# Stepped weight tiles in the up and gate products, and permuted moving columns in the second block

## The chip, the cores and the metric

The kernel is one program on one core of a Trainium2 chip. The metric is the device time of that program in microseconds; the kernel before was run twice. TensorE (PE) multiplies: a weight load (PEld in the profile) brings 128 columns of a stationary operand into the array, and a matmul streams the moving operand past them into a PSUM bank. ACT (ScalarE) and DVE (VectorE) prepare operands and empty banks, SP issues the DMAs.

## The reference, cut to what matters

Two networks follow one another on 256 tokens of width 2048, in float32: first two layers with mixers, an FFN with a convolution and an embedding gate, then two layers with three kinds of attention. The change touches these products:

```python
# first block, in each of two layers
h = causal_dwconv(x @ w_up, conv_w, conv_b)          # up0, up1: 2048 x 11264
gate, up = jnp.split(h, 2, axis=-1)
y = (jax.nn.gelu(gate) * up) @ w_down                # down0, down1: untouched
x = x + jax.nn.sigmoid(x @ ple_w_gate[layer]) * (p[layer] @ ple_w_proj[layer])   # pg0, pg1: 2048 x 2048
# second block, in each of two layers
proj = jnp.einsum('bsd,de->bse', h, w_in[l])         # in20 then ib0, in21 then ib1
```

## The kernel before, in words

**Layout.** Activations lie with features on the partitions: a matrix of 2048 features is 16 tiles of 128 partitions x 256 tokens. A weight matrix is cut into pieces of 256 output columns; a piece in DRAM is 128 partitions x 4096 words, which are 16 tiles (one per 128 input features) of 256 columns. A piece arrives in one of three slots of `ring` by a DMA of SP. It has two halves of 128 output columns; each half becomes one output tile.

**Precision.** Each f32 operand is split into a high part, rounded to fp32r, and a low part, the remainder. ACT writes the high part of a half (line 1771), DVE the low part (line 2506, a helper that `split` on line 2564 calls). Both read the half's 128 columns out of the 256 of each tile and write them without gaps, so that `WHI[half]` and `WLO[half]` are 16 tiles of 128 x 128 words, one after the other. The input has a high and a low part likewise, `rhi` and `rlo`, which lie apart in SBUF.

**The matmuls.** `wide_half` (from line 821) makes one half. It waits for a free bank and for the half's high part (`w_hi`), then runs 16 matmuls on line 863: the high weights against the high and the low input together, 512 moving columns, which `pair` describes as two runs of 256. The bank's 512 columns take the two sums. It waits for the low part (`w_lo`) and runs 16 matmuls on line 849 (`from_low_weights`): the low weights against the high input, 256 columns, added to the main half of the bank. ACT and DVE then add the two halves of the bank up. In front of each matmul stands the load of its weights; the program writes the two as one `mm`.

**Which halves.** `up0` and `up1` have 44 pieces each, `pg0` and `pg1` 8, `ib0` and `ib1` 17. The first piece of `up` and `pg` goes through `both_halves` instead, because its input arrives in quarters: 96 matmuls of 256 columns on lines 885, 891 and 897. All others of these names go through `wide_half`. For `up` the pieces run in a hardware loop of three (`rounds`). In the second block, small jobs (logits, transposes, attention values) stand between the halves of `ib0` and `ib1`.

**Order.** SP loads a piece as soon as the slot's last reader has signalled (`piece_done`). ACT splits a half as soon as the piece is there and PE has finished the earlier half in that place (`g_done`), DVE follows ACT, PE follows both.

**Other places that the text speaks of.** Line 2811 is a DVE copy of 32 words per partition, each the last of 64 (`XT[..., C - 1]`), so 64 words apart. Line 1555 has attention logits and line 1679 transposes, with 128 moving columns and plain f32 operands; line 1181 has weights of 32 columns.

Of the kernel before, what the change touches and what calls it, by code (L numbers as in the profile page):

```python
# [15 lines left out]
P = 128  # L16
D = 2048
DT = D // P
# [75 lines left out]

EV_TILES = [24, 25, 26] + list(range(8, 16)) + list(range(0, 8)) + list(range(16, 24))
EV_HALVES = 16 + len(EV_TILES)


def place(p):
# [125 lines left out]
def build(nc, dram, out):  # L225
# [38 lines left out]
    with ctx:  # L264
# [280 lines left out]
        def parts_of(name):  # L545

            return (2, 3, 0, 1) if name == "ev_out" else (0, 1, 2, 3)

        def halves_of(name):

            return (DHI, DLO, FC) if name[:4] == "down" else (WHI, WLO, DT)
# [27 lines left out]
        def pair(name, kk):  # L579

            if name[:4] == "down":
                a, b = kk, FT + high_slot(kk)
                return scrv[:, a:b + 1:b - a, :]
            a, b = sorted(at_ // T + kk for at_ in HI_LO[name])
            if name not in SOURCE:
                a, b = a - 2 * X // T, b - 2 * X // T
                return scrv[:, a:b + 1:b - a, :]
            return allv[:, a:b + 1:b - a, :]
# [171 lines left out]
        def _(pe):  # L760
            mm = nc.tensor.matmul
# [59 lines left out]
            def wide_half(name, k, half, i, first=False, count=1):  # L821

                _, rhi, rlo = RHS[name]
                u = wide_unit(name, k, half)
                b = unit_bank(u)
                main, low = sums(b, name)

                pe.wait_ge(bank_free[u % R3], i * 4 + (2 * (u // R3) + 2))
                pe.wait_ge(S["w_hi"], at(HALF0[name] + half + 1, k, i, 2))
                early = 12  # L830

                def from_high(first_, last):
                    for kk in range(first_, last):
                        if kk % 4 == 0:
                            pe.wait_ge(S["r_hi"], 4 * R_SPLIT.index(name) + kk // 4 + 1)
                        mm(main, WHI[half][:, kk, :], rhi[:, kk, :], start=kk == 0, stop=False,
                           skip_group_check=True)

                def from_low(first_, last):
                    for kk in range(first_, last):  # L840
                        if kk % 4 == 0:
                            pe.wait_ge(S["r_lo"], 4 * R_SPLIT.index(name) + kk // 4 + 1)
                        last_ = mm(low, WHI[half][:, kk, :], rlo[:, kk, :], start=False, stop=False,
                                   skip_group_check=True)
                    return last_

                def from_low_weights(first_, last):
                    for kk in range(first_, last):
                        last_ = mm(main, WLO[half][:, kk, :], rhi[:, kk, :], start=False, stop=kk == DT - 1,  # L849
                                   skip_group_check=True)  # L850
                    return last_

                if first:
                    from_high(0, early)
                    from_low(0, early)
                    pe.wait_ge(S["w_lo"], at(HALF0[name] + half + 1, k, i, 2))
                    from_low_weights(0, early)
                    from_high(early, DT)
                    from_low_weights(early, DT)
                    one = from_low(early, DT)  # L860
                else:
                    for kk in range(DT):
                        mm(b[:, :], WHI[half][:, kk, :], pair(name, kk), start=kk == 0, stop=False,  # L863
                           skip_group_check=True)
                    pe.wait_ge(S["w_lo"], at(HALF0[name] + half + 1, k, i, 2))
                    one = from_low_weights(0, DT)
                one.then_inc(S["g_done"], count)

            def both_halves(name, high, low, units):

                n, first = R_SPLIT.index(name), HALF0[name]
                _, rhi, rlo = RHS[name]
                whi, wlo = zip(*(first_weights(name, half) for half in range(2)))
                for u in units:
                    pe.wait_ge(bank_free[u % R3], 2 * (u // R3) + 2)
                pe.wait_ge(S["w_hi"], first + 2)
                pe.wait_ge(S["w_lo"], first + (2 if name in FIRST_SECOND_HALF else 1))

                def tiles_of(part):
                    return range(4 * part, 4 * part + 4)  # L880

                def high_high(half, part):
                    pe.wait_ge(S["r_hi"], 4 * n + part + 1)
                    for kk in tiles_of(part):
                        mm(high[half], whi[half][:, kk, :], rhi[:, kk, :], start=kk == 0, stop=False, skip_group_check=True)

                def low_high(half, part):
                    if half and not part:
                        pe.wait_ge(S["w_lo"], first + 2)
                    for kk in tiles_of(part):  # L890
                        mm(high[half], wlo[half][:, kk, :], rhi[:, kk, :], start=False, stop=kk == DT - 1,
                           skip_group_check=True)

                def high_low(half, part):
                    pe.wait_ge(S["r_lo"], 4 * n + part + 1)
                    for kk in tiles_of(part):
                        one = mm(low[half], whi[half][:, kk, :], rlo[:, kk, :], start=False, stop=kk == DT - 1,
                                 skip_group_check=True)
                    return one

                def from_high(part):
                    for half in range(2):
                        high_high(half, part)
                    for half in range(2):
                        low_high(half, part)

                from_high(0)
                for half in range(2):
                    high_low(half, 0)
                from_high(1)  # L910
                for half in range(2):
                    high_low(half, 1)
                from_high(2)
                high_high(0, 3)
                low_high(0, 3)
                high_low(0, 2)
                high_low(0, 3).then_inc(S["g_done"], 1)
                high_high(1, 3)
                low_high(1, 3)
                high_low(1, 2)  # L920
                high_low(1, 3).then_inc(S["g_done"], 1)
# [2631 lines left out]
    return np.ascontiguousarray(w.transpose(3, 0, 2, 1, 4).reshape(-1, P, kt * cols))  # L3553


def _half_tiled(w):

    w = _tiled(w, 4, 512)
    return np.ascontiguousarray(w.reshape(-1, 2, P, 2048).transpose(0, 2, 1, 3).reshape(-1, P, 4096))
# [11 lines left out]
def _matrices():  # L3571
    f = np.float32
    out = np.zeros((P, NMAT), f)
    i = np.arange(P)

    def put(name, a):
        out[:a.shape[0], MCOL[name]:MCOL[name] + a.shape[1]] = a

    put("ident", np.eye(P, dtype=f))
    put("ones", np.ones((P, P), f))  # L3580
    put("bones", (i[:, None] // 64 == i[None, :] // 64).astype(f))
    put("rswap", (i[:, None] == (i[None, :] ^ 32)).astype(f))
    j = np.arange(C)
    r = i % C
    sel = np.zeros((P, 32), f)
    sel[i, i // 64] = 1
    put("sel", sel)
    put("selt", ((i[:, None] % 32 < 2) & (i[:, None] % 32 == i[None, :] // 64)).astype(f))
    put("mask", np.concatenate([r[:, None] < j[None, :], r[:, None] <= j[None, :]], 1).astype(f))
    put("twice", (r[:, None] == j[None, :]).astype(f))  # L3590
    levels = []
    for lv in range(6):
        s = 1 << lv

        levels.append(((r[:, None] // (2 * s) == j[None, :] // (2 * s)) & (j[None, :] // s % 2 == 1)
                       & (r[:, None] // s % 2 == 0)).astype(f))
    put("lmask", np.concatenate(levels, 1))

    rel = np.arange(384) - 255
    n = np.abs(rel)  # L3600
    large = 8 + sum((n * n >= 64 * (1 << k)).astype(int) for k in range(1, 8))
    bucket = np.where(rel > 0, 16, 0) + np.where(n < 8, n, np.minimum(large, 15))
    put("onehot", (np.arange(32)[:, None] == bucket[None, :]).astype(f))
    return out


def _layout(a):

    ev, od = a["ev_w_in"][0], a["od_w_in"][0]
    d = {}  # L3610
# [70 lines left out]
    }  # L3681
    d["vec"] = np.ascontiguousarray(np.concatenate([part[name] for name, _ in VECS], 1))
    d["mat"] = _matrices()
    d["relb"] = np.ascontiguousarray(a["rel_bias"])
    pos = np.asarray(a["positions_2"]).astype(np.int32)
    d["posi"] = np.ascontiguousarray(np.concatenate([np.repeat(pos[None], P, 0), pos.reshape(2, P).T], 1))
# [19 lines left out]
```

## Time and profile before

| | us |
|---|---|
| the two runs | 3287.78, 3289.35 |
| median | 3288.57 |
| span of the profiled execution, first to last instruction | 3284.6 |
| PE busy in that span | 3232.2 |
| weight loads busy | 2855.1 |
| DVE busy | 2195.8 |
| ACT busy | 1667.5 |

The profile has no other time for the profiled execution than its span; the runs are 3.2 and 4.8 us longer. Busy time is the union of the records of an engine. Matmuls and weight loads are pipelined: a record of some 390 ns is the latency of one matmul, while the next one starts earlier. How fast they follow one another is read from the chain (so many in so many us), not from the mean of one.

### The profile page before, as it was taken

What the parts mean: (1) busy time and instruction counts of PE and PEld (TensorE: products, weight loads), DVE (VectorE), ACT (ScalarE), POOL (GpSimd) and SP (SyncE); (2) the same over time, 40 slices, a digit from 0 to 9 for tenths busy, and PEclk for the clock granted to TensorE, in tenths of its full rate; (3) what the DMA queues carried; (4) which work ended last, traced back from release to release, by engine and by line L of the source; (5) the groups of instructions that cost most, each with busy time, mean ns of one, the idle gap of its engine ahead of it and who ended that gap; (6) DMA issues with size and microseconds to landing.
All of it is one profiled execution on the core that took longest, in us unless ns stands there. A gap on an engine that the chain in (4) does not pass through costs nothing.

```text
span 3284.6 us, 53186 instructions
## 1 busy us (share of the span) xinstructions
PE 3232.2 (98%) x21672; PEld 2855.1 (87%) x21672; DVE 2195.8 (67%) x2836; ACT 1667.5 (51%) x2138; POOL 24.5 (1%) x38
## 2 busy tenths in 40 slices
PE   9999999999999999999999999999999999999998
PEld 8888898888888888888888888888888888888887
DVE  6577767666676456676766666745675767647676
ACT  5574346555554335554555555533564456444563
POOL 0000000000000000011000000000000000000000
PEclk9999999999999999999999999999999999999999
DMA  7352145455444554534445445455544434444342
GB/s 279 143 210 67 57 167 200 181 188 196 179 185 175 184 190 183 190 119 180 164 181 199 182 186 198 159 186 192 188 168 185 171 129 167 186 175 167 129 171 112
DMA packets 47254, 563.64 MB, mean 172 GB/s; under 512 B 5072, under 2 KB 7264, under 8 KB 10720
## 3 DMA queue, kind: packets, MB, share of 16 engines
q1 hardware_dynamic: 47072, 561.06, 45.4%
q8 instruction: 133, 2.18, 0.3%
q14 instruction: 49, 0.40, 0.0%
HBM read 558.92 MB, written 2.12 MB: 171 GB/s over the span
## 4 chain that ended last, share of the span: by engine, by line
PE 90%; DVE 5%; ACT 3%; issue 2%; DMA 0%; SPq 0%; DVEq 0%; ACTq 0%
PE bank L863 40%; PE bank L849 21%; PE bank L968 10%; PE bank L973 5%; PE bank L1002 3%; ACT spl_r L1771 1%; PE bank L1468 1%; DVE ring L2506 1%; PE bank L784 1%; PE bank L788 1%; PE bank L782 1%; DVE spl_r L2506 1%; DVE xb L2506 1%; DVE xa L2506 0%; DVE scr L2506 0%
## 5 line engine op out<-in xcount | busy, mean ns | idle before, releaser
L2506 DVE TENSOR_TENSOR spl_r<-ring,spl_r 128x2048 fp32r<-128x2048 f32 (+2 forms) x429 | 961.3, 2242 | 485.8 <-ACT spl_r L1771 480.8
L863 PE MATMUL bank<-all_r,spl_r 128*128 128x512 f32 x4960 | 1196.6, 393 | 3.2 <-ACT spl_r L1771 3.2
L1771 ACT ACTIVATE spl_r<-ring 128x2048 fp32r<-128x2048 f32 x407 | 779.2, 1915 | 591.0 <-PE bank L849 484.1
L863 PEld LDWEIGHTS bank<-all_r,spl_r 128*128 128x128 f32 x4960 | 914.5, 188 | 189.5 <-issue 8.0
L849 PEld LDWEIGHTS bank<-all_r,spl_r 128*128 128x128 f32 x5008 | 642.1, 191 | 24.2
L849 PE MATMUL bank<-all_r,spl_r 128*128 128x256 f32 x5008 | 650.0, 283 | 0.0
L2506 DVE TENSOR_TENSOR dsp_r<-ring,dsp_r 128x1408 fp32r<-128x1408 f32 x126 | 204.8, 1625 | 206.4 <-ACT dsp_r L1771 206.2
L968 PE MATMUL bank<-scr_r,dsp_r 128*128 128x512 f32 x1386 | 338.8, 392 | 0.0
L1771 ACT ACTIVATE dsp_r<-ring 128x1408 fp32r<-128x1408 f32 x126 | 174.4, 1384 | 283.3 <-PE bank L973 283.1
L968 PEld LDWEIGHTS bank<-scr_r,dsp_r 128*128 128x128 f32 x1386 | 252.5, 189 | 47.4
L863 PE MATMUL bank<-scr_r,spl_r 128*128 128x512 f32 x1152 | 275.8, 391 | 2.9 <-ACT spl_r L1771 2.9
L863 PEld LDWEIGHTS bank<-scr_r,spl_r 128*128 128x128 f32 x1152 | 211.7, 188 | 45.0 <-issue 3.8
L2512 DVE SCALAR_TENSOR_TENSOR xtra<-sumbuf,vec,xtra 128x255 f32<-128x255 f32 (+1 forms) x352 | 170.2, 484 | 102.0 <-ACT xtra L1929 66.7
L973 PEld LDWEIGHTS bank<-scr_r,dsp_r 128*128 128x128 f32 x1386 | 182.9, 191 | 9.8
L1929 ACT ACTIVATE xtra<-sumbuf,vec 128x256 f32<-128x256 f32 x176 | 105.0, 598 | 168.1 <-DVE sumbuf L2506 168.1
L973 PE MATMUL bank<-scr_r,dsp_r 128*128 128x256 f32 x1386 | 185.9, 282 | 0.0
L849 PEld LDWEIGHTS bank<-scr_r,spl_r 128*128 128x128 f32 x1184 | 151.8, 191 | 5.6
L849 PE MATMUL bank<-scr_r,spl_r 128*128 128x256 f32 x1184 | 153.9, 283 | 0.0
L1935 ACT ACTIVATE xtra<-xtra 128x256 f32<-128x256 f32 x88 | 36.9, 419 | 160.5 <-DVE xtra L2512 160.5
L2506 DVE TENSOR_TENSOR sumbuf<-bank,sumbuf 128x256 f32<-128x256 f32 x275 | 114.7, 418 | 3.9 <-ACT sumbuf L1813 3.7
L1813 ACT ACTIVATE sumbuf<-bank 128x256 f32<-128x256 f32 x275 | 100.2, 365 | 15.6 <-PE bank L849 15.6
L2506 DVE TENSOR_TENSOR scr<-xtra 128x256 f32 (+1 forms) x88 | 37.5, 426 | 18.7 <-DVE xtra L2512 18.4
(437 smaller groups left out, 2673.9 us busy)
## 6 DMA issues: line engine op xcount, KB each, us to landing
ring<-in_up SPq DMA_DIRECT2D x88, 2048.0 KB, 7.8
ring<-in_down SPq DMA_DIRECT2D x64, 1408.0 KB, 6.0
ring<-in_ib SPq DMA_DIRECT2D x34, 2048.0 KB, 7.8
ring<-in_pg SPq DMA_DIRECT2D x16, 2048.0 KB, 7.8
ring<-in_out SPq DMA_DIRECT2D x16, 2048.0 KB, 7.9
ring<-in_in SPq DMA_DIRECT2D x12, 2048.0 KB, 7.7
ring<-in_ec SPq DMA_DIRECT2D x11, 2048.0 KB, 8.4
ring<-in_ea SPq DMA_DIRECT2D x8, 2048.0 KB, 10.5
```

The costliest lines, as they stand in the source:

```text
L782: mm(out_, WHI[half][:, kk, :], rhi[:, kk, :], start=kk == tile_order[0], stop=False)
L849: last_ = mm(main, WLO[half][:, kk, :], rhi[:, kk, :], start=False, stop=kk == DT - 1, skip_group_check=True)
L863: mm(b[:, :], WHI[half][:, kk, :], pair(name, kk), start=kk == 0, stop=False, skip_group_check=True)
L968: mm(b[:, :], high[:, kk, :], pair(name, piece * FC + kk), start=piece + kk == 0, stop=False, skip_group_check=True)
L973: one = mm(main, low[:, kk, :], HHI[:, high_slot(piece * FC + kk), :], start=False, stop=piece == 3 and kk == FC - 1, skip_group_check=True)
L1002: one = mm(out, lhsT, rhs, start=n == 0, stop=n == len(terms) - 1)
L1771: A(high[half], w[:, :, half * P:(half + 1) * P], ACT.Copy).then_inc(S["w_hi"], count)
L1813: A(dst, shape(sums(b, name)[1]), ACT.Copy).then_inc(S["low_act"], count)
L1929: one = A(GU[:, k % R3, half, :], SU[:, k % R3, half, :], ACT.Identity, bias=pick(v("cb", col, FT), index(k, i)), scale=pick(v("cw2", col, ...
L1935: A(GU[:, k % R3, 0, :], GU[:, k % R3, 0, :], ACT.Gelu_apprx_tanh).then_inc(S["up_gelu"], 1)
L2506: return V.tensor_tensor(out, a, b, op)
L2512: return V.scalar_tensor_tensor(out=out, in0=a, scalar=s, in1=b, op0=op0, op1=op1)
```

## The change

Weight tiles of four products are stored interleaved. With a step of n, the tiles of a half lie in groups of n, and the columns of one tile are n words apart: word c * n + j of a group is column c of its tile j. `_stepped` lays the weights out so on the host, and `stationary` reads a tile with that step: 2 words in `up0`, 16 in `up1`, 4 in `pg0`, 8 in `pg1`. All other products keep a step of 1. In `ib0` the moving columns and the bank's columns are both taken from last to first, within each run of 256, in all matmuls. In `ib1` the matmuls of 256 columns (the low weights) take columns in fours, first the fours of even number, then those of odd number, in the input and in the bank alike; its matmuls of 512 columns stay.

```diff
+STEPS = {"up0": 2, "up1": 16, "pg0": 4, "pg1": 8}
...
+        def stationary(name, part, kk):
+
+            step = STEPS.get(name, 1)
+            group = part[:, kk - kk % step:kk - kk % step + step, :].rearrange("p x n -> p (x n)")
+            return group[:, kk % step::step]
+
+        def lines(name, ap):
+
+            if name == "ib1":
+                return ap.rearrange("p (m x c) -> p x m c", x=2, c=4)
+            return ap[:, ::-1] if name == "ib0" else ap
+
+        def both_sides(name, b, kk):
+
+            if name != "ib0":
+                return b[:, :], pair(name, kk)
+            return b[:, :].rearrange("p (x t) -> p x t", x=2)[:, :, ::-1], pair(name, kk)[:, :, ::-1]
...
                 def from_low_weights(first_, last):
                     for kk in range(first_, last):
-                        last_ = mm(main, WLO[half][:, kk, :], rhi[:, kk, :], start=False, stop=kk == DT - 1,
-                                   skip_group_check=True)
+                        last_ = mm(lines(name, main), stationary(name, WLO[half], kk), lines(name, rhi[:, kk, :]), start=False,
+                                   stop=kk == DT - 1, skip_group_check=True)
                     return last_
...
                     for kk in range(DT):
-                        mm(b[:, :], WHI[half][:, kk, :], pair(name, kk), start=kk == 0, stop=False,
+                        both, x = both_sides(name, b, kk)
+                        mm(both, stationary(name, WHI[half], kk), x, start=kk == 0, stop=False,
                            skip_group_check=True)
...
                     for kk in tiles_of(part):
-                        mm(high[half], wlo[half][:, kk, :], rhi[:, kk, :], start=False, stop=kk == DT - 1,
+                        mm(high[half], stationary(name, wlo[half], kk), rhi[:, kk, :], start=False, stop=kk == DT - 1,
                            skip_group_check=True)
...
+def _stepped(d):
+
+    for name, step in STEPS.items():
+        n = step
+        w = d[name].reshape(-1, P, 16 // n, n, 2, P)
+        w = w.transpose(0, 1, 2, 4, 5, 3).reshape(-1, P, 16 // n, 2, n, P).transpose(0, 1, 2, 4, 3, 5)
+        d[name] = np.ascontiguousarray(w).reshape(d[name].shape)
```

The other matmuls of `wide_half` and `both_halves` that take weights take them through `stationary` in the same way.

## Rows read from the trace of the kernel before

**Rows 1.** The page: engines, granted clock by slice, chain that ended last
```profile
PE 3232.2 (98%) x21672; PEld 2855.1 (87%) x21672; DVE 2195.8 (67%) x2836; ACT 1667.5 (51%) x2138; POOL 24.5 (1%) x38
...
PEclk9999999999999999999999999999999999999999
...
PE 90%; DVE 5%; ACT 3%; issue 2%; DMA 0%; SPq 0%; DVEq 0%; ACTq 0%
PE bank L863 40%; PE bank L849 21%; PE bank L968 10%; PE bank L973 5%; PE bank L1002 3%; ACT spl_r L1771 1%; PE bank L1468 1%; DVE ring L2506 1%; PE bank L784 1%; PE bank L788 1%; PE bank L782 1%; DVE spl_r L2506 1%; DVE xb L2506 1%; DVE xa L2506 0%; DVE scr L2506 0%
```

**Rows 2.** The chain, one half of up0: start us, us, what
```profile
898.23 3.65 PE bank L863 x16
901.88 1.91 PE bank L849 x16
```

**Rows 3.** Busy time by stretch: opening and rest of up0, pg0, up1, pg1; ib0, ib1
```profile
core 0: us, PE busy (x) PEld busy (x) DVE busy (x) ACT busy (x) POOL busy (x), PEclk, DMA share, GB/s
506.30:519.40 13.10, 12.40 (x96) 11.67 (x96) 9.63 (x10) 10.71 (x17) 0.00 (x0) 1.00 0.66 281
519.40:999.00 479.60, 479.29 (x2753) 423.45 (x2754) 333.43 (x391) 253.14 (x305) 0.00 (x0) 1.00 0.49 184
1259.60:1273.30 13.70, 12.42 (x96) 11.70 (x96) 10.15 (x11) 10.73 (x16) 0.00 (x0) 1.00 0.69 289
1273.30:1351.80 78.50, 78.44 (x450) 69.25 (x451) 51.87 (x49) 40.65 (x51) 0.00 (x0) 1.00 0.51 188
1604.70:1617.90 13.20, 13.04 (x97) 12.85 (x97) 9.69 (x11) 10.77 (x17) 0.00 (x0) 0.89 0.65 276
1617.90:2097.40 479.50, 479.21 (x2753) 423.34 (x2754) 333.34 (x391) 253.04 (x305) 0.00 (x0) 1.00 0.49 184
2358.10:2371.60 13.50, 13.45 (x96) 13.05 (x96) 10.12 (x11) 10.55 (x16) 0.00 (x0) 0.87 0.68 290
2371.80:2450.90 79.10, 78.38 (x449) 69.10 (x450) 57.41 (x66) 45.47 (x58) 0.00 (x0) 1.00 0.49 186
2549.60:2742.50 192.90, 192.82 (x1105) 168.32 (x1104) 141.22 (x247) 104.25 (x195) 0.00 (x0) 1.00 0.38 144
2959.20:3152.00 192.80, 192.72 (x1105) 168.23 (x1104) 141.50 (x247) 104.53 (x195) 0.00 (x0) 1.00 0.38 144
```

**Rows 4.** Groups in up0, 519.4 to 999 us: xcount, busy us, mean ns, idle
```profile
L863 PE MATMUL bank<-all_r,spl_r 128*128 128x512 f32 x1376 | 328.4, 391 | 0.4 <-ACT spl_r L1771 0.4
L849 PE MATMUL bank<-all_r,spl_r 128*128 128x256 f32 x1376 | 178.5, 283 | 0.0
...
L849 PEld LDWEIGHTS bank<-all_r,spl_r 128*128 128x128 f32 x1376 | 176.4, 191 | 6.7
```

**Rows 5.** Weight loads of other sizes and kinds, whole span, by form
```profile
L1679 PEld LDWEIGHTS bank<-mat,scr 128*128 128x128 f32 x128 | 15.2, 141 | 5.5 <-issue 2.6 <-DVE scr L2512 0.6
...
L1555 PEld LDWEIGHTS bank<-scr 128*128 128x128 f32 x64 | 9.2, 191 | 3.1 <-issue 2.9
...
L1181 PEld LDWEIGHTS bank<-xb,mat 128*32 128x32 f32 x32 | 0.8, 109 | 0.2
```

**Rows 6.** Timeline, weight loads from 1471.0 us: start us, us, xcount
```profile
1471.08 0.19 PEld L1555 LDWEIGHTS bank<-scr 128*128 128x128 f32 x1 [0.24 <-issue]
...
1471.19 0.30 PEld L1555 LDWEIGHTS bank<-scr 128*128 128x128 f32 x2
```

**Rows 7.** DVE groups by form: 256 words, 8 words, and the stepped copy
```profile
L2506 DVE TENSOR_TENSOR scr<-xtra 128x256 f32 x78 | 33.2, 426 | 18.4 <-DVE xtra L2512 18.4
...
L2506 DVE TENSOR_TENSOR spl<-spl 128x8 f32<-128x8 f32 x10 | 1.7, 168 | 0.3
...
L2811 DVE COPY pc<-xtra 128x32 f32<-128x32 f32 x1 | 0.2, 191 | 0.0
```

**Rows 8.** Groups in pg0, 1273.3 to 1351.8 us; then in ib0, 2549 to 2742.5 us
```profile
L849 PE MATMUL bank<-scr_r,spl_r 128*128 128x256 f32 x224 | 29.1, 283 | 0.0
...
L863 PE MATMUL bank<-all_r,spl_r 128*128 128x512 f32 x432 | 107.3, 400 | 0.0
```

More of the change, by code:

```diff
@@ L835, in from_high @@
                             pe.wait_ge(S["r_hi"], 4 * R_SPLIT.index(name) + kk // 4 + 1)
-                        mm(main, WHI[half][:, kk, :], rhi[:, kk, :], start=kk == 0, stop=False,
+                        mm(main, stationary(name, WHI[half], kk), rhi[:, kk, :], start=kk == 0, stop=False,
                            skip_group_check=True)
@@ L842, in from_low @@
                             pe.wait_ge(S["r_lo"], 4 * R_SPLIT.index(name) + kk // 4 + 1)
-                        last_ = mm(low, WHI[half][:, kk, :], rlo[:, kk, :], start=False, stop=False,
+                        last_ = mm(low, stationary(name, WHI[half], kk), rlo[:, kk, :], start=False, stop=False,
                                    skip_group_check=True)
@@ L884, in high_high @@
                     for kk in tiles_of(part):
-                        mm(high[half], whi[half][:, kk, :], rhi[:, kk, :], start=kk == 0, stop=False, skip_group_check=True)
+                        mm(high[half], stationary(name, whi[half], kk), rhi[:, kk, :], start=kk == 0, stop=False, skip_group_check=True)
                 def low_high(half, part):
@@ L896, in high_low @@
                     for kk in tiles_of(part):
-                        one = mm(low[half], whi[half][:, kk, :], rlo[:, kk, :], start=False, stop=kk == DT - 1,
+                        one = mm(low[half], stationary(name, whi[half], kk), rlo[:, kk, :], start=False, stop=kk == DT - 1,
                                  skip_group_check=True)
@@ L3683, in _layout @@
     d["mat"] = _matrices()
+    _stepped(d)
     d["relb"] = np.ascontiguousarray(a["rel_bias"])
```

## The prediction

> **What bounds the kernel now.** Read the page first, then the chain, then the steady stretch, then the stages. TensorE is busy for 98% of the span, every slice shows a granted clock of nine tenths or more, and the chain that ends last lies on PE for 90% of the span, most of it on lines 863 and 849, the two loops of `wide_half` [rows 1]. A tile of weights meets the inputs twice there: high part of the weights against both parts of the input (512 moving columns), then low part against the high part (256 columns). In the steady stretch a half piece costs 3.65 + 1.91 us, with nothing between [rows 2]: 16 matmuls of 512 columns at 0.228 us and 16 of 256 columns at 0.119 us. So 256 more columns cost (3.65 - 1.91)/16 = 0.109 us, 0.425 ns a column, and what is left of either is about 0.01 us a matmul. The granted clock is 1.00 in the long stretches that the change touches, the upper of the two levels (2.4 GHz), and 0.89 and 0.87 over the opening pieces of up1 and pg1 [rows 3]. PE has nearly no idle time in the long ones: 479.29 us busy of 479.60 in the first expansion, where PE waits 0.4 us for the split of its weights [rows 3, 4]. DVE (333 us) and ACT (253 us) follow PE and have slack. So every nanosecond that an instruction of TensorE gets longer is seen in the time, unless it is a weight load that still fits under the matmul that runs beside it; and nothing outside TensorE can gain or lose.
>
> The span is 3284.6 us; the two runs took 3287.78 and 3289.35 us, so 4.0 us lie around the span up to their median, 3288.57. I add my terms to the median.
>
> **What doesn't change.** No instruction is added or removed: the 21672 matmuls and weight loads stay. The new order of the weight words is made on the host. The DMAs carry the same pieces in the same shape, and ACT's rounding and DVE's subtraction (lines 1771 and 2506) still read and write whole halves in their old order. No wait is added and no queue reordered. A half is waited for as a whole before its first tile is read, also in the opening pieces, so the fact that a stepped tile touches words spread over up to 16 tiles adds no wait. The permutation of the moving columns is the same on the input and on the bank, so evictions are as before. What remains is how TensorE's reads and writes walk.
>
> **Weight loads.** A load takes 109 ns for 32 columns and 191 for 128 [rows 5]: (191 - 109)/96 = 0.85 ns a column, some 109 ns for 128 by that slope, and a latency of 82 ns that is pipelined. Two loads have started 0.11 us apart where matmuls are short [rows 6]. So the load's own pace is about 0.11 us, as the slope says. Beside a 512-column matmul (0.228 us) it has 0.12 us to spare; beside a 256-column one (0.119 us) only 0.01 us. The cover is thick in one loop, paper-thin in the other: a load twice as slow would disappear in the first and stand almost full in the second, +0.10 us each. The loads beside 256-column matmuls: up0 and up1 have 86 halves x 16 = 1376 each [rows 4] and 96 in the opening piece, 1472; pg0 and pg1 have 14 x 16 + 96 = 320 each [rows 3, 8].
> - up1 (step 16 words): nothing, to 1472 x 0.10 = +147 us.
> - pg0 (4) and pg1 (8): nothing, to 320 x 0.10 = +32 us each.
> - up0 (2): nothing, to +147 us.
> A gain is excluded: the load must still bring 128 columns, the clock is at its top, and beside 512 columns a shorter load shows nowhere.
>
> No PE row shows a step. Two rows are near. First, a transposing load brings its 128 f32 columns in 141 ns, not 191 [rows 5]: over the same 82 ns that is 0.46 ns a column. The read side can thus deliver more than a plain load takes, which needs one column per 0.85 ns; there is reserve of nearly two. That reserve is seen on neighbouring words alone. Second, the only stepped read in the trace: the copy of line 2811 takes 32 columns, 64 words apart (the last column of each chunk), in 191 ns. DVE's operations on 8 neighbouring words take 168 ns and those on 256 take 426 ns: (426 - 168)/248 = 1.04 ns a word [rows 7]. The stepped copy's 24 words beyond 8 cost 191 - 168 = 23 ns, 0.96 ns each: the pace of neighbouring words. At half pace it would have been some 33 ns longer. So one word per 1.04 ns from far apart costs nothing; the load needs one per 0.85 ns, a fifth faster. I take nothing for all four steps, as nearest to this row, and keep the upper ends.
>
> The Trainium skill speaks against this: in "Advanced Engine Details and Errata", section "Memory Cachelines", SBUF is said to work in lines of 16 bytes, of which two accesses in a row must hit the same one to hide the SRAM's latency. By that a step of 2 words is free and 4, 8 and 16 are not; with a halved pace the sum would be that of the first rival below. The copy of line 2811 hits a new line with every word and shows no such penalty at DVE's pace; at the load's pace no row shows it.
>
> **Moving columns.** A matmul streams a column in 0.425 ns, so here the read side is at twice the load's pace, and no row has a stepped read at it. Backwards: neighbours still follow one another, only in falling order, and the bank is written falling too. Even fours first: four neighbours, then a jump over four, on both sides. The rows nearest are the two-tile reads of line 863, which jump between two stretches of 256 words without visible cost: 512 columns cost no more than 256 by the column price above plus 0.01 us [rows 2]. Bounds: ib0 has 34 halves, 544 matmuls of each size (27 of the 34 halves lie in the window [rows 8]); half pace would add 544 x (0.218 + 0.109) = +178 us. For ib1 only the 256-column matmuls are touched: 544 x 0.109 = +59 us. Value taken: nothing for both, by the same stepped copy, which paid for no jump, and by the two-tile reads; this is a choice, as both rows are far.
>
> **Sum:** 3288.6 + 0 = 3289 us.
>
> **Rivals.**
> 1. *The far steps halve the load's pace (slower).* Place: line 849 and the opening pieces of up1, pg0, pg1. Price 0.10 us x (1472 + 320 + 320) = 211 us: 3500 us (3494 to 3519 with 0.097 to 0.109 us). It decides from the point where a load's own pace passes 0.12 us, some 10% above today's 0.11. For it: that thin cover, and that no row shows a load stepping. Against it: the stepped copy, and the reserve of the transposing load. If step 2 were slowed too, 3647 us. The opening pieces have waits of their own (12.40 us busy of 13.10 [rows 3]), which hide little. Line 863 would stay at 0.228 us, as 0.11 + 0.109 is still below it.
> 2. *Backwards costs (slower).* Each column of ib0 is fetched or written alone, at half pace: +178 us, 3466 us. For it: this is the fast stream with no reserve on view, and reading and writing are turned together. Against it: nothing more is touched than before. The Trainium skill says of PSUM, in the same section, that pairs of neighbouring elements should stay together and that other patterns slow matmuls much; falling pairs keep together, so I read it as no cost, but no row here shows it.
> 3. *Several at once*: 1 and 2 give 3288.6 + 211 + 178 = 3678 us; with up0 and ib1 as well, 3884 us.
> 4. *A nibble:* loads grow by 20 ns (half passes the cover): 10 ns x 2112 = 21 us, 3310 us. Within 2% (66 us), which is about what this measurement tells from no change.
>
> That the change doesn't do what it says has little room: a step is either in the read pattern of each load or it isn't.
>
> **Chances.** No cost anywhere 0.48, the nibble 0.07, rival 1 0.22, rival 2 0.12, several or all 0.11. Faster by over 2%: 0.01, for what I don't see. Within 2%: 0.54. Slower: 0.45. The range must take in rivals 1 and 2 to leave only the several out: 3283 to 3520 us. The likeliest case's own range is 3284 to 3312 us.
>
> **What would show it.** Right: the four windows of the up and gate stages keep their lengths (479.6, 78.5, 479.5 and 79.1 us), a half keeps 3.65 + 1.91 us, and the weight loads beside 256 columns keep 191 ns. Rival 1: in up1 the second number of a half grows to about 3.5 us while the first stays, the mean load grows from 191 towards 300 ns, and up0 keeps its length. Rival 2: in ib0 3.65 grows towards 7.1 and 1.91 to 3.65, in ib1 neither. The forecast is wrong if up1 is longer than up0 by over 30 us, or the window of ib0 longer than that of ib1 by as much; today both pairs are equal within 0.1 us [rows 3].

## The result, and the profile after

The changed kernel took 3534.02 us (3533.65 and 3534.38), 245.5 us more than the 3288.57 of before: a ratio of 1.0748, 95% interval 1.0717 to 1.0779. The forecast of no change was wrong; the time lies 14 us above the upper end of the range and 34 us above the first rival. The span of the profiled execution is 3531.8 us, 247.2 us more. Line numbers move with the edits: 863 and 849 of before are 885 and 870 here and 881 to 886 and 866 to 871 in the experiments; 2506 is 2528, 1771 is 1793, 1679 is 1698 and 2811 is 2833 there. First the page: engines and chain.

```profile
PE 3482.6 (99%) x21672; PEld 3181.0 (90%) x21672; DVE 2196.0 (62%) x2836; ACT 1668.3 (47%) x2138; POOL 24.5 (1%) x38
...
PE 93%; DVE 3%; ACT 2%; issue 1%; DMA 0%; SPq 0%; DVEq 0%; ACTq 0%
```

Against [rows 1] the counts are the same, DVE and ACT are busy for the same time, PE for 250.3 us more and the weight loads for 325.9 us more. Now the same stretches as in [rows 3], in the same order: opening and rest of up0, pg0, up1, pg1, then ib0 and ib1 (us; busy time and count of PE, PEld, DVE, ACT, POOL; clock; DMA share; GB/s).

```profile
507.50:520.60 13.10, 12.43 (x96) 11.74 (x96) 9.61 (x10) 10.70 (x17) 0.00 (x0) 1.00 0.66 281
520.60:1010.20 489.60, 489.53 (x2753) 435.34 (x2754) 333.38 (x391) 253.21 (x305) 0.00 (x0) 1.00 0.48 180
1270.80:1293.30 22.50, 22.49 (x97) 22.50 (x97) 11.58 (x12) 10.90 (x16) 0.00 (x0) 1.00 0.41 174
1293.30:1398.20 104.90, 104.90 (x449) 104.90 (x449) 51.53 (x50) 40.84 (x50) 0.00 (x0) 1.00 0.38 141
1651.00:1672.50 21.50, 21.49 (x96) 21.50 (x97) 10.97 (x11) 10.96 (x17) 0.00 (x0) 0.92 0.41 172
1672.50:2305.40 632.90, 632.90 (x2753) 632.90 (x2753) 332.26 (x391) 253.02 (x304) 0.00 (x0) 1.00 0.37 139
2566.30:2589.50 23.20, 23.20 (x96) 23.20 (x97) 11.63 (x12) 10.84 (x16) 0.00 (x0) 0.93 0.40 168
2589.50:2698.80 109.30, 109.30 (x451) 109.27 (x451) 58.08 (x67) 45.54 (x58) 0.00 (x0) 1.00 0.36 135
2796.40:2991.00 194.60, 194.58 (x1107) 168.02 (x1105) 141.53 (x248) 104.62 (x195) 0.00 (x0) 1.00 0.38 143
3207.30:3399.70 192.40, 192.29 (x1107) 167.61 (x1105) 141.76 (x248) 104.93 (x195) 0.00 (x0) 1.00 0.38 144
```

Opening and rest together: up0 (step 2) 10.0 us more, pg0 (4) 35.2, up1 (16) 161.7, pg1 (8) 39.9; ib0 1.7 more, ib1 0.4 less. Together these are 248.1 us, beside 247.2 for the span: all the rest of the kernel is the same within 1 us. In the three stages with steps of 4 and more the loads have no pause any longer: PEld is busy for 632.90 of 632.90 us in up1, where it had 56 us of pauses. The chain shows a half of up1, then one of up0, then in pg1 the second part of a half and the first part of the next (start us, us, what), beside 3.65 and 1.91 us in [rows 2]:

```profile
1702.10 3.90 PE bank L885 x16
1706.01 3.46 PE bank L870 x16
...
600.48 3.77 PE bank L885 x16
604.25 1.92 PE bank L870 x16
...
2601.51 3.75 PE bank L870 x16
2605.26 4.05 PE bank L885 x16
```

In up1 the second part grows by 1.55 us, 0.097 us a matmul, and the first by 0.25. Of this 0.25 nearly half is one interval: the second matmul of 512 columns of a half starts 0.349 us after the first, 0.233 before (medians of the 86 halves). One load of high weights still meets a matmul of 256 columns there: in experiment 5 that interval is 0.338 us where the high weights alone are stepped, 0.232 where the low ones alone are. The other intervals of 512 columns are 0.237 us, and 0.236 in up0, where no first interval stands out; before, 0.228. The loads beside 512 columns, ns min/median/max, in up0, pg0, up1 and pg1 (before, a mean of 188 on line 863 beside 512 columns, and [rows 4] shows 191 on line 849, beside 256):

```profile
L885 PEld LDWEIGHTS bank<-all_r,spl_r x1376: 193/196/198, 520.6 to 1007.7; 128*128 128x128 f32 x197
...
L885 PEld LDWEIGHTS bank<-scr_r,spl_r x224: 308/310/330, 1293.2 to 1394.1; 128*128 128x128 f32 x112
...
L885 PEld LDWEIGHTS bank<-all_r,spl_r x1376: 297/302/323, 1672.4 to 2301.5; 128*128 128x128 f32 x197
...
L885 PEld LDWEIGHTS bank<-scr_r,spl_r x224: 322/332/342, 2589.4 to 2694.3; 128*128 128x128 f32 x112
```

Over the latency of 82 ns taken from [rows 5], a column of the load costs 0.89 ns with step 2, 1.78 with 4, 1.72 with 16 and 1.95 with 8. The pace says nearly the same without that latency: beside 256 columns the loads start 0.233 us apart with step 4, 0.223 with 16 and 0.241 with 8, which is 1.82, 1.74 and 1.88 ns a column.

### The profile page after: what moved, and what is told of

It is laid out like the page before. It is cut to its first block, busy times and chain, and to the rows that moved or that the text cites. A ratio compares the mean times of both kernels' runs of the same rounds, so it can differ in the third digit from the quotient of the medians.

```text
span 3531.8 us, 53186 instructions
## 1 busy us (share of the span) xinstructions
PE 3482.6 (99%) x21672; PEld 3181.0 (90%) x21672; DVE 2196.0 (62%) x2836; ACT 1668.3 (47%) x2138; POOL 24.5 (1%) x38
## 4 chain that ended last, share of the span: by engine, by line
PE 93%; DVE 3%; ACT 2%; issue 1%; DMA 0%; SPq 0%; DVEq 0%; ACTq 0%
PE bank L885 39%; PE bank L870 25%; PE bank L990 9%; PE bank L995 5%; PE bank L1024 3%; PE bank L1490 1%; ACT spl_r L1793 1%; PE bank L907 1%; PE bank L919 1%; PE bank L805 1%; PE bank L809 1%; PE bank L803 1%; PE bank L913 1%; DVE ring L2528 1%; PE bank L1701 0%
## 5 line engine op out<-in xcount | busy, mean ns | idle before, releaser
L885 PE MATMUL bank<-all_r,spl_r 128*128 128x512 f32 x4960 | 1231.5, 401 | 2.5 <-ACT spl_r L1793 2.4
L885 PEld LDWEIGHTS bank<-all_r,spl_r 128*128 128x128 f32 x4960 | 1005.5, 223 | 139.9 <-issue 8.0
L870 PEld LDWEIGHTS bank<-all_r,spl_r 128*128 128x128 f32 x5008 | 780.0, 225 | 18.1
L870 PE MATMUL bank<-all_r,spl_r 128*128 128x256 f32 x5008 | 781.6, 309 | 0.0
L885 PE MATMUL bank<-scr_r,spl_r 128*128 128x512 f32 x1152 | 284.0, 399 | 1.7 <-ACT spl_r L1793 1.7
L885 PEld LDWEIGHTS bank<-scr_r,spl_r 128*128 128x128 f32 x1152 | 239.7, 240 | 27.0 <-issue 1.8
L870 PEld LDWEIGHTS bank<-scr_r,spl_r 128*128 128x128 f32 x1184 | 203.1, 244 | 3.4
L870 PE MATMUL bank<-scr_r,spl_r 128*128 128x256 f32 x1184 | 203.3, 324 | 0.0
```

The lines of the kernel that those rows point to most:

```text
L870: last_ = mm(lines(name, main), stationary(name, WLO[half], kk), lines(name, rhi[:, kk, :]), start=False, stop=kk == DT - 1, skip_group_ch ...
L885: mm(both, stationary(name, WHI[half], kk), x, start=kk == 0, stop=False, skip_group_check=True)
```

## The experiments

Runs of before on the same chips took 3282.94 to 3289.51 us. Where one run of a kernel is told, the stretches of its profile carry the reading, not the total. The edits are cut to the lines that matter.

**1 and 2. The two parts of the change, each alone.**

```diff
# e1_weights: lines() and both_sides() return their operands straight
+            return ap
...
+            return b[:, :], pair(name, kk)
# e2_moving
+STEPS = {}
```

> The four steps of the change stay, the moving columns of ib0 and ib1 are read forwards as before. Theory A (nearly all of the loss is in the weight loads): up0 489.6, pg0 104.9, up1 632.9, pg1 109.3 us as in the changed kernel, and ib0 back from 194.6 to 192.9, ib1 from 192.4 to 192.8; the whole about 3533 us. Rival B (the permuted columns cost something elsewhere too, or slow the weight stages through shared memory): over 10 us less than 3534.

> No step on any weight tile, only the permuted moving columns. Theory A: +1.7 us in ib0, -0.5 to -0.9 us in ib1, so 3288 to 3291 us, not told from before. Rival B (order of the columns costs at the fast stream's pace, hidden in the changed kernel by something): above 3300 us.

The weights alone gave 3529.94 us, 243 more than the 3286.53 of before on that chip, with 489.40, 104.90, 632.90 and 109.00 us in the four long stretches. The moving columns alone gave 3285.58 us against 3286.53: ratio 0.9999, 0.9989 to 1.0008. So the loss is in the weight loads; backwards and fours together cost or give nothing that the total shows.

**3. Does the cost belong to the step or to the stage?** Here the four names trade their steps.

```diff
+STEPS = {"up0": 8, "up1": 4, "pg0": 16, "pg1": 2}
```

> The steps trade places: up0 8 (was 2), up1 4 (was 16), pg0 16 (was 4), pg1 2 (was 8); moving columns forwards. Theory A (the cost belongs to the step: 0.226 us from load to load with 4, 0.233 with 8, 0.216 with 16): up0 about 43 x 2 halves x (4.05 + 3.74) = 670 us, up1 86 x (3.88 + 3.62) = 645 us, pg0 14 x (3.90 + 3.46) = 103 us, pg1 14 x (3.77 + 1.92) = 80 us. Rival B (the cost belongs to the stage and what runs beside it on ACT, DVE and the DMAs): 16 in pg0 costs what 8 or 4 cost there (105 us or more), and up1 keeps 633 us.

The long stretches of up0, pg0, up1 and pg1:

```profile
529.50:1199.10 669.60, 669.60 (x2753) 669.60 (x2753) 332.20 (x391) 257.41 (x304) 0.00 (x0) 1.00 0.35 132
1481.40:1584.50 103.10, 103.10 (x450) 103.10 (x450) 51.74 (x50) 40.65 (x50) 0.00 (x0) 1.00 0.39 143
1859.90:2504.30 644.40, 644.40 (x2753) 644.40 (x2753) 332.31 (x391) 254.32 (x304) 0.00 (x0) 1.00 0.36 137
2778.80:2859.20 80.40, 79.82 (x448) 70.92 (x449) 57.53 (x66) 45.53 (x58) 0.00 (x0) 1.00 0.48 183
```

669.6, 103.1, 644.4 and 80.4 us where 670, 103, 645 and 80 were expected: the step alone sets the price, what runs beside it doesn't.

**4. Steps between and beyond.**

```diff
+STEPS = {"up0": 3, "up1": 5, "pg0": 7, "pg1": 12}   # groups of as many tiles; a rest keeps step 1
```

> Steps that are no powers of two: up0 3, up1 5, pg0 7, pg1 12 words (tiles that don't fill a group keep a step of 1: one of 16 with 3 and 5, two with 7, four with 12); moving columns forwards. Theory L (each 16-byte line that is opened costs about 1.80 ns, words of the same line 0.85 at least): step 3 opens 3 lines for 4 words, 1.35 ns a column, load 252 ns, 256-column matmuls 0.168 us apart, a half 3.70 + 2.7 us; step 5 opens a line with every word, load 302 to 331 ns, 3.4 to 3.7 us for the second part. Rival S (a threshold: up to 3 words apart is free, from 4 on all cost): step 3 like step 2, 195 ns and 1.92 us. Rival T (threshold above 2 words, 8 bytes): step 3 like step 4, 310 ns and 3.5 us.

A half of up0 (step 3), then the loads beside 512 columns in up0, up1, pg0 and pg1:

```profile
900.40 3.81 PE bank L885 x16
904.21 2.70 PE bank L870 x16
```

```profile
L885 PEld LDWEIGHTS bank<-all_r,spl_r x1376: 187/252/263, 522.7 to 1079.3; 128*128 128x128 f32 x197
...
L885 PEld LDWEIGHTS bank<-all_r,spl_r x1376: 187/306/323, 1740.8 to 2366.2; 128*128 128x128 f32 x197
...
L885 PEld LDWEIGHTS bank<-scr_r,spl_r x224: 187/312/335, 1364.2 to 1463.0; 128*128 128x128 f32 x112
...
L885 PEld LDWEIGHTS bank<-scr_r,spl_r x224: 187/368/373, 2653.0 to 2759.0; 128*128 128x128 f32 x112
```

Step 3 stands where the count of opened lines (of four words each) puts it: 252 ns and 2.70 us. Both thresholds (1.92 or 3.5 us) fall. Steps 5 and 7 cost what 4 costs; 12 costs more, 368 ns, which a flat price a line doesn't give. The shortest loads, 187 ns, are those of the tiles left at step 1.

**5. One side stepped alone.** In up0 only the high weights (beside 512 columns), in up1 only the low weights (beside 256), with step 16; weights are stored plainly, so both products are not the reference's.

```diff
+            return part.rearrange("p x n -> p (x n)")[:, kk::16]   # high in up0, low in up1
```

> Weights stored plainly; in up0 only the high weights (beside 512 columns) are read with a step of 16 words, in up1 only the low weights (beside 256 columns); so up0 and up1 are not the reference's products. Theory A (a stepped load is seen in full beside 256 columns, and beside 512 adds 0.010 to 0.016 us to the matmul it runs under): up0's halves 3.90 + 1.91 us, the stretch 86 x 5.81 = 500 us against 479.6; up1's halves 3.65 + 3.46 us, 611 us. Rival B (the growth beside 512 columns is only the tail of the slow 256-column part, a queue that empties): up0 stays at 480 us, and up1 takes the whole 633 us.

A half of up0, then one of up1:

```profile
902.28 3.87 PE bank L886 x16
906.15 1.91 PE bank L871 x16
...
2000.65 3.67 PE bank L886 x16
2004.32 3.46 PE bank L871 x16
```

The two costs are apart. The load, with a median of 301 ns beside 512 columns, is covered but for 0.22 us a half (up0 497.4 us, 500 expected); the same load beside 256 columns costs the whole 1.55 us (up1 613.0 us, 611 expected). Rival B falls.

**6. Other readers with far steps.** Transposing loads, DVE's subtraction for pg0 and ACT's rounding for pg1 (attention of the second block, pg0 and pg1 are not the reference's).

```diff
+   src[:, 2 * q + x::4] if l == 0 else src[:, q * T + x:(q + 1) * T:2]                      # transposes
...
+   src = slot_of(g)[:, 0:2048].rearrange("p (m s) -> p s m", s=16)                          # DVE pg0, ACT pg1
```

> Weights plain. Other readers get far steps: the transposing loads of the second block (line of P2) a step of 4 words in layer 0 and 2 in layer 1, DVE's subtraction for pg0 and ACT's rounding for pg1 each read 2048 words with a step of 16 words (attention of the second block, pg0 and pg1 are then not the reference's). Theory L (PE's load port pays 1.80 ns for each 16-byte line opened, whatever the kind of load): transposing loads 82 + 128 x 1.8 = 312 ns with step 4 and some 197 ns with step 2, from 141 ns; the reserve of the transposing load was only that of words in one line. Rival W (a plain load reads each word twice, high and low, and pays 0.9 ns a line): 197 ns with step 4, 141 ns with step 2. DVE and ACT: by the copy of line 2811 unchanged, 2292 and 1915 ns; by the port's price of 1.80 ns for each word 3700 ns or more each.

Transposing loads with step 4, then with step 2; then DVE in pg0 and ACT in pg1 (busy us, mean ns):

```profile
L1698 PEld LDWEIGHTS bank<-mat,scr x64: 195/208/218, 2625.1 to 2770.7; 128*128 128x128 f32 x64
...
L1698 PEld LDWEIGHTS bank<-mat,scr x64: 194/203/218, 3035.4 to 3181.0; 128*128 128x128 f32 x64
...
L2528 DVE TENSOR_TENSOR spl_r<-ring,spl_r 128x2048 fp32r<-128x2048 f32 x15 | 55.2, 3680 | 15.2 <-ACT spl_r L1793 15.2
...
L1793 ACT ACTIVATE spl_r<-ring 128x2048 fp32r<-128x2048 f32 x17 | 58.7, 3453 | 1.8 <-PE bank L915 1.8
```

DVE needs 3680 ns instead of 2291, 1.8 ns a word (2048 x 1.8 = 3686); ACT's mean goes from 1914 to 3453 ns, with the opening halves, which were read straight, in it. So with a step of 16 a word costs both of these readers about 1.8 ns, as it costs the plain load, and the copy of line 2811 had told nothing of it. The total rose by 41 us, as the splits became what pg0 and pg1 wait for. The transposing load fits neither theory whole: 203 ns with step 2, near theory L's 197, and 208 with step 4, where L has 312 and W 197. That is 0.95 to 0.98 ns a column, twice its pace with neighbours (141 ns). Its reserve is gone at the first step, and the step of 4 adds next to nothing.

**7 to 9. The moving side.** First steps inside each run of 256 words of the input, the bank in order (the tokens come out permuted, so not the reference's).

```diff
+        INPUT = {"up0": 2, "up1": 4, "pg0": 8, "pg1": 16}
...
+            return ap if n == 1 else ap.rearrange("p (m x) -> p x m", x=n)
```

> Weights plain. The moving columns are read with a step inside each run of 256 words, the bank written in order: up0 2 words, up1 4, pg0 8, pg1 16 (tokens come out permuted in these products, so the result is not the reference's). Theory L (1.80 ns a line on the moving side too): step 2 0.90 ns a column, 512-column matmuls 0.46 to 0.48 us apart and 256-column ones 0.24 us, a half 11.3 us and up0 some 970 us; steps 4 to 16 1.80 ns a column, a half 22.5 us, up1 some 1930 us. Rival M (the moving port opens a line in half the time, 0.85 ns, as it streams columns in half the time of a load): step 2 free (479.6 us), step 4 0.85 to 0.9 ns a column, up1 some 950 us.

A half of up0 (step 2), then of up1 (step 4):

```profile
902.50 7.22 PE bank L884 x16
909.71 3.63 PE bank L869 x16
...
2510.25 7.38 PE bank L884 x16
2517.63 3.73 PE bank L869 x16
```

Both theories miss a part. Step 2 already costs nearly all that is paid with any step here, 0.451 us a matmul of 512 columns and 0.88 ns a column, as L said, where M had it free; step 4 costs 0.461, as M said, where L had 0.92. The stretches are 935.8 and 955.8 us. With 8 and 16 the ones of pg0 and pg1 are 145.4 and 146.4 us, less than twice before. Then runs of words, on both sides, in the matmuls of 256 columns of every product:

```diff
+        RUN = {"up1": 8, "pg0": 32, "pg1": 64, "ib1": 2}
...
+            return ap.rearrange("p (m x c) -> p x m c", x=2, c=RUN.get(name, 4))
```

> Weights plain, all matmuls of 256 columns in every product of wide_half take their columns in two interleaved sets of runs: runs of 8 in up1, 32 in pg0, 64 in pg1, 2 in ib1, 4 everywhere else (up0, ib0, the input and output products). In the changed kernel the 16 such matmuls of a half of ib1 took 1.88 us, before 1.91. Theory G (a run order other than straight saves 2 ns a matmul between one accumulation and the next on the same bank): 0.03 us x about 387 halves = 12 us less than before, 0.4%. Rival N (the 0.03 us belong to ib1's surroundings): same as before within 3 us, and up0 keeps 3.65 + 1.91.

It took 3335.38 us, ratio 1.0147 (1.0130 to 1.0164), where 12 us less than before had been expected. up0 and up1 (runs of 4 and 8) fell to 476.6 us each. pg0 and pg1 (runs of 32 and 64) gained nothing, 1.92 and 1.91 us for the second part. In ib1, with runs of 2, the second part takes 3.45 us for 15 matmuls, 0.23 us each, twice as long. A half of pg0, then one of ib1:

```profile
1300.43 3.67 PE bank L883 x16
1304.10 1.92 PE bank L868 x16
...
3103.00 3.67 PE bank L883 x16
3106.67 3.45 PE bank L868 x15
```

Theory G holds for runs of 4 and 8 and fails for the others. To see which side pays, and which gives, one side alone was permuted; the same kernel has a near copy on line 2811.

```diff
+        INPUT, BANK = {"up0": (2, 2), "up1": (2, 4), "pg1": (2, 8)}, {"ib1": (2, 2), "ib0": (2, 4)}
...
+            return ap.rearrange("p (m x c) -> p x m c", x=x, c=c)
# the copy of line 2811 reads 32 neighbouring words
```

> Weights plain, matmuls of 512 columns straight. In the matmuls of 256 columns one side alone is permuted (tokens then come out in another order, not the reference's): the input in two sets of runs of 2 words in up0, of 4 in up1, of 8 in pg1; the bank in runs of 2 in ib1 and of 4 in ib0. The copy of line 2811 reads 32 neighbouring words (its products are then not the reference's). Theory R (the input side pays for a 16-byte line that yields two words only): up0's second part 3.68 us as in ib1 of the run before, up0 about 631 us, and ib1 1.9. Rival K (the bank side pays): ib1's second part 3.68 us, up0 477 to 480 us. Gain of 0.03 us: if it belongs to the input side, up1 476.6 us and ib0 1.91; if to the bank side, up1 479.4 and ib0 1.88. Copy: if a far word costs 1.8 ns and a near one 1.04, the near copy takes 191 - 24 = 167 ns; if the copy paid nothing for its step, 191 ns.

The stretches of up0 (input in runs of 2) and up1 (runs of 4), then the copy:

```profile
521.40:1151.00 629.60, 629.60 (x2752) 544.37 (x2753) 333.49 (x391) 252.98 (x305) 0.00 (x0) 1.00 0.37 140
1771.50:2248.10 476.60, 476.25 (x2752) 420.44 (x2753) 333.30 (x391) 253.00 (x305) 0.00 (x0) 1.00 0.49 185
```

```profile
L2833 DVE COPY pc<-xtra 128x32 f32<-128x32 f32 x1 | 0.2, 174 | 0.0
```

The input pays for runs of 2 (629.6 us, 631 expected) and gives the 0.03 us with runs of 4; in ib1 and ib0, where the bank alone was permuted, 16 matmuls keep 1.91 us. The near copy takes 174 ns: the far one of [rows 7], 191 ns, seems to have paid 17. Each run has one record of it; in the twelve runs with the far copy it took 183 to 198 ns, so all of them are above the near one, and the size of what was paid is anything from 9 to 24 ns.

**10. The gain by itself.** The runs point to a version that beats both kernels: plain weights, even fours first on both sides in all matmuls of 256 columns of `wide_half` and of the down products.

```diff
+STEPS = {}
...
+            return ap.rearrange("p (m x c) -> p x m c", x=2, c=4)
...
-                                one = mm(main, low[:, kk, :], HHI[:, high_slot(piece * FC + kk), :], start=False,
+                                one = mm(lines(name, main), low[:, kk, :], lines(name, HHI[:, high_slot(piece * FC + kk), :]), start=False,
```

> Weights plain, all matmuls of 256 columns of wide_half and of the down products take their columns even fours first, on both sides; nothing in runs of 2. From the run before: 0.03 us less in each of about 387 halves, 12 us, and 0.03 x 87 = 3 us in the down products: 3272 to 3275 us beside 3287, a ratio of 0.995 to 0.996. If the down products, whose low weights have 11 tiles a piece, gain nothing: 3275. Rival: the total stays within 0.1% of before because the other engines' pace takes the gain back in the second block.

```profile
902.54 3.65 PE bank L881 x16
906.20 1.88 PE bank L866 x16
```

The median of five runs is 3271.28 us, against 3285.58 of before on that chip: ratio 0.9955, 0.9941 to 0.9969. That is 14.3 us, with 12 to 15 expected at 0.03 us a half.

**11. More distances.**

```diff
+STEPS = {"up0": 6, "up1": 9, "pg0": 10, "pg1": 14}
```

> Weight tiles with steps of 6 (up0), 9 (up1), 10 (pg0) and 14 words (pg1), in groups of as many tiles; the rest of the 16 tiles keeps a step of 1 (4, 7, 6 and 2 tiles). Each opens a new 16-byte line with every word. Theory L (1.80 ns for each line opened, and multiples of 4 words apart from it for another reason): loads of 302 to 315 ns beside 512 columns in all four, 223 to 234 ns apart beside 256 columns. Rival B (the distance in lines matters: 3 lines cost most, 368 ns with 12 words; 2 lines 331 ns with 8; 1 and 4 lines least): 10 words (2.5 lines) and 9 (2.25 lines) come near 331 ns or above, 14 (3.5 lines) between 302 and 368 ns, 6 (1.5 lines) near 310.

The loads beside 512 columns had medians of 304 ns (6), 318 (9), 324 (10) and 326 (14). These medians are over all 16 tiles of a half, of which 4, 7, 6 and 2 are not stepped; for the stepped tiles alone they are 307, 325, 330 and 327 ns. Theory L (302 to 315 ns in all four) holds for 6 words only. Rival B comes out: 310 expected for 6, 331 or so for 9 and 10, and between 302 and 368 for 14. So the distance matters, with 3 lines (12 words) the worst and 4 lines (16 words) the best. Why, is open.

## Why the prediction was wrong, point by point

- *What bounds the kernel, and the cover.* Right: the loss is all on TensorE, and it is seen where the cover is thin. The load's own pace, 0.11 us, the 0.12 us to spare beside 512 columns and the 0.01 beside 256 gave rival 1's second part of about 3.5 us, for 3.46 measured. Experiment 5 showed the two covers apart.
- *The step that failed:* "I take nothing for all four steps, as nearest to this row", resting on the stepped copy of line 2811. Its 191 ns were compared with operations of other kinds on 8 words. The same copy with near words took 174 ns (experiment 9), so it had paid some 17 ns and not nothing, and from run to run it varies by 15 ns. A single record of 32 words, read through another kind's start-up, couldn't carry a price per word; over 2048 words DVE paid 3680 ns for 2291 (experiment 6). What was put at nothing cost 133 us in the second parts of up1 alone (86 halves x 1.55 us). I also chose between ends 211 us apart by a row whose uncertainty was the whole effect.
- *The reserve of the transposing load* was no reserve: with a step of 2 that load took 203 ns for 141 (experiment 6), and a plain load with a step of 4 takes 310 for 188.
- *Weight loads, term by term.* Upper ends taken for rival 1: 147 us for up1, 32 for pg0 and for pg1, none for up0. Measured: 161.7, 35.2, 39.9 and 10.0. Two things were missing. Beside 512 columns a stepped load lengthens the matmul, although the load itself is covered: from 0.228 us to 0.236 with step 2 and 0.237 with 16. That is 0.12 us a half in up0, which is all of its loss, and about 0.13 in up1; with 8 words, in pg1, it is more (4.05 us for 16, against 3.65). And the price beside 256 columns was put at 0.10 us a load, which makes 0.22 us from load to load; it is 0.223 with 16, 0.233 with 4 and 0.241 with 8.
- *Moving columns.* Right in the sum: +1.7 us in ib0 and -0.4 in ib1, ratio 0.9999 for both. But it was luck. The reason given was that the stepped copy and the two-tile reads pay for no jump; by it the same input in runs of 2, or with a step of 2, would be free too, and these take twice the time (experiments 7 and 9).
- *The Trainium skill.* Its rule in "Advanced Engine Details and Errata", "Memory Cachelines", was weighed against the copy, and the copy was believed. The loads of this change follow it: step 2 nearly free (196 ns for 188), from 4 words on a penalty (302 to 332 ns). The moving columns and transposing loads don't: two accesses to the same 16 bytes (step 2, or runs of 2) already cost the double (experiments 6, 7 and 9). Of PSUM the Trainium skill says in the same section that any pattern that is not contiguous slows matmuls much; banks written in runs of 2 or 4 kept 1.91 us here (experiment 9), and ib0, written backwards, took 1.7 us more in 194.6.
- *The range* ended at 3520, 20 us above rival 1's 3500. The two missing terms are some 36 us over that rival (10.0 in up0, 15 in up1, 3 in pg0, 8 in pg1), and so beyond the range.

## What to carry to other kernels

Before a load is called hidden, compare its pace with the shortest matmul that it runs beside, and ask what any lengthening would do there. Keep f32 operands of TensorE in whole runs of four neighbouring words: the stationary side bears a step of 2 for little, the moving side bears none. A price per word is read from a long operation of the same kind, or measured; a bound of 200 us isn't closed with one short record.

## What the runs showed of the hardware that was not expected

- Plain weight loads of 128 columns, f32 in the profile, beside 512 columns and of the stepped tiles alone, by step in words: 188 ns (1), 196 (2), 252 (3), 310 (4), 306 (5), 307 (6), 312 (7), 332 (8), 325 (9), 330 (10), 368 (12), 327 (14), 302 (16). Counted in lines of four words, one price of some 1.8 ns for each line opened fits 2 to 7 and 16, with 0.85 ns a column as the least for 1; the excess of 8 to 14 stays open.
- Moving columns of fp32r: 0.425 ns with neighbours, 0.88 ns with step 2 and 0.90 with 4, so no second doubling. Transposing loads do the same (141, 203, 208 ns). Why these two stop near 0.9 ns and the plain load, DVE and ACT go to 1.8 ns a word isn't settled by these runs.
- Even fours first is faster than straight order by 0.03 us in 16 matmuls of 256 columns, and it is the reading of the input that gives it: 0.4% of the kernel. Runs of 8 give the same, runs of 32 and 64 nothing (experiment 8). No run tells why.
